# A streaming encoder step: unit 0's product block by block, and six low halves moved from GpSimd to VectorE

## The reference, cut to what matters

```
h = RMSNorm(x); z = h @ w_in                      # 9216 columns: GLU a, b, q, k, v, two gates
conv branch: GLU, causal depthwise conv 31, LayerNorm, swish, @ w_conv_out
attention:   8 heads, differential, QK-RMSNorm, rotary, block-causal mask, @ w_attn_out
x = x + (sigmoid(gate_conv) * conv + sigmoid(gate_attn) * attn) @ w_out
h2 = RMSNorm(x); q = h2 @ w_pq                    # 8 heads x 128
s1, s2 = q halves against 128 keys each           # top 16 of each, top 16 of the 256 sums
y = x + sum over the 16 chosen of softmax(score) * gelu(h2 . u_tab[idx]) * v_tab[idx]
```

## Time and profile before

| | |
|---|---|
| median of 3 runs | 4030.99 us (4030.02 to 4040.12) |
| the profiled execution, its own time | 4019.61 us |
| its span | 4017.8 us |
| mean granted TensorE clock | 0.981 of full |
| TensorE matmuls busy | 3831.1 us, 95% |
| VectorE busy | 3046.7 us, 76% |
| ScalarE busy | 1099.1 us, 27% |
| GpSimd busy | 1364.6 us, 34% |

### The profile page before, as it was taken

The page is one execution under the profiler, slowest core; times in us unless marked ns, Lnnn a source line. Parts: engine busy times, 40 slices in busy tenths (PEclk is TensorE's granted clock), DMA queues, the critical chain, the costliest instruction groups (busy, mean ns, idle before and its releaser), DMA issues.

```text
span 4017.8 us, 67592 instructions
## 1 busy us (share of the span) xinstructions
PE 3831.1 (95%) x24995; PEld 3772.7 (94%) x24995; DVE 3046.7 (76%) x3852; ACT 1099.1 (27%) x1126; POOL 1364.6 (34%) x947
## 2 busy tenths in 40 slices
PE   8989989989989998999999999999999999999999
PEld 7889889988989998998999999999999999999999
DVE  6887887788776424188668999998678888888876
ACT  3223222222323112132223333333222222222222
POOL 3333333333334442466652222222223333233320
PEclk9999999999989999999999999999999999999999
DMA  7998999989978997786759999999979888889895
GB/s 283 320 347 316 322 321 327 330 306 338 350 267 294 324 329 251 253 294 229 242 214 352 383 386 389 382 387 380 355 272 357 338 334 337 341 321 347 330 355 188
DMA packets 451684, 1285.17 MB, mean 320 GB/s; under 512 B 34368, under 2 KB 258368, under 8 KB 343360
## 3 DMA queue, kind: packets, MB, share of 16 engines
q1 hardware_dynamic: 372576, 876.99, 61.5%
q0 software_dynamic: 46080, 335.56, 21.2%
q10 hardware_dynamic: 32832, 70.07, 4.5%
HBM read 1070.18 MB, written 345.75 MB: 352 GB/s over the span
## 4 chain that ended last, share of the span: by engine, by line
PE 51%; issue 15%; DMA 13%; DVE 11%; POOL 5%; SPq 3%; ACT 1%; DVEq 1%; POOLq 0%; ACTq 0%
PE ST L1889 18%; PE ST L1800 17%; PE PA L1560 13%; DMA u_rows<-u_out 6%; POOL w_lo L622 5%; DMA w_raw<-w_all 4%; DVE xg L1069 4%; DMA rows<-v_rows,v_idx 2%; PE ST L1865 2%; DVE u_out L968 2%; SPq L393 1%; DVE w_lo L1364 1%; DVE PA L1459 1%; ACT w_hi L677 1%; DMA rows<-u_rows,v_idx 1%
## 5 line engine op out<-in xcount | busy, mean ns | idle before, releaser
L622 POOL TENSOR_TENSOR w_lo<-w_raw,w_hi 128x512 fp32r<-128x512 f32 x612 | 838.3, 1402 | 1223.4 <-ACT w_hi L677 1223.4
L677 ACT ACTIVATE w_hi<-w_raw 128x2048 fp32r<-128x2048 f32 x368 | 703.6, 1912 | 1307.3 <-PE ST L1889 507.2
L1889 PE MATMUL ST<-wt_hi,w_hi 128*128 128x384 f32 x2048 | 686.9, 335 | 15.2 <-DVE w_lo L1364 15.1
L1889 PE MATMUL ST<-wt_lo,w_hi 128*128 128x384 f32 x2048 | 684.7, 334 | 0.0
L1889 PE MATMUL ST<-wt_hi,w_lo 128*128 128x384 f32 x2048 | 684.7, 334 | 0.0
L1364 DVE TENSOR_TENSOR w_lo<-w_raw,w_hi 128x2048 fp32r<-128x2048 f32 x213 | 487.1, 2287 | 174.1 <-ACT w_hi L677 166.8
L650 POOL DMA_INDIRECT rows<-v_rows,v_idx x160 | 322.9, 2018 | 739.3 <-DVE PA L1459 670.2
L1560 PE MATMUL PA<-h_hi,w_hi 128*128 128x272 f32 x2496 | 547.8, 301 | 6.4 <-POOL w_lo L622 6.4
L1560 PE MATMUL PA<-h_hi,w_lo 128*128 128x272 f32 x2496 | 527.1, 293 | 0.0
L1560 PE MATMUL PA<-h_lo,w_hi 128*128 128x272 f32 x2496 | 527.1, 293 | 0.0
L1800 PE MATMUL ST<-h_hi,w_hi 128*128 128x384 f32 x1408 | 508.5, 361 | 2.2 <-ACT h_b L875 1.6
(11 more groups left out here) (271 smaller groups left out, 6190.6 us busy)
## 6 DMA issues: line engine op xcount, KB each, us to landing
w_raw<-w_all SPq DMA_DIRECT2D x368, 1024.0 KB
u_in<-w_all SPq DMA_DIRECT2D x128, 1024.0 KB, 8.7
u_rows<-u_out SPq DMA_DIRECT2D x512, 256.0 KB, 7.5
v_rows<-w_all SPq DMA_DIRECT2D x128, 1024.0 KB, 9.2
a_scr<-gb ACTq DMA_DIRECT2D x128, 192.0 KB
g_scr<-g_st ACTq DMA_DIRECT2D x24, 1024.0 KB, 11.9
gl_st<-g_scr SPq DMA_DIRECT2D x30, 768.0 KB
a_st<-a_scr SPq DMA_DIRECT2D x30, 768.0 KB
```

The lines of the kernel that those rows point to most:

```text
L622: ins = pool.tensor_tensor(w_lo[:, slot, cols], raw[:, slot, cols], w_hi[:, slot, cols].bitcast(F32), ALU.subtract)
L677: act.activation(w_hi[:, slot, :], raw[:, slot, :], ACT.Copy).then_inc(hi_ready, 1)
L1889: last = mm(PB[n % 2][:, k, :], a, r_[b][:, c, :], start=(c == 0 and y == 0), stop=(c == GRP - 1 and y == 2))
```

## The change

At the start: SyncE's queue loads the constants behind the first piece of x and unit 0; ScalarE's queue keeps parameters and lambdas, with a semaphore of their own, and makes one small copy ahead of the data. GpSimd no longer makes squares or low halves there: ScalarE makes the even squares, VectorE the odd ones and the low halves of units 0 and 1. TensorE starts unit 0 once its low half and the first `h_lo` are there, waits per block, and takes the sums of squares in four lots, behind blocks 4, 8, 11 and 13. The hooks `stats` and `rot` of the first head move one quarter of a unit later. Later: VectorE makes the low half of the third query unit behind its first two copies, and in each top-k tile that of the last unit (7), between the multiply and the reduction of list 0. GpSimd's loops are cut at these units.

```diff
@@ SyncE
             for i in range(4):
                 sp.dma_start(xs[:, 4 * i:4 * i + 4, :], x_t[:, 4 * i:4 * i + 4, :]).then_inc(x_loaded[i], 16)
-                if i == 1:
+                if i == 0:
                     load_w(0, 0)
+                    sp.dma_start(cst[:, :], consts).then_inc(const_loaded, 16)
             load_w(0, 1)
@@ GpSimd
-            for k in range(1, KD, 2):
-                pool.wait_ge(x_loaded[k // 4], 16)
-                pool.tensor_tensor(xsq[:, k, :], xs[:, k, :], xs[:, k, :], ALU.mult).then_inc(xsq_pool, 1)
-                if k == KD // 2 - 1:
-                    lo_whole(0, 0)
-            lo_whole(1, 1)
...
+            pool.wait_ge(lo_ready, 2)
+            made = 0
+            for w0, w1 in ((2, U_PQ + 2), (U_PQ + 3, U_PU + TOPK_UNITS - 1), *((U_PU + TOPK_UNITS * t, U_PU + TOPK_UNITS * (t + 1) - 1)
+                                                                   for t in range(1, TT)), (U_PU + TOPK_UNITS * TT, U_PU + U_G0 + 1)):
+                pool.wait_ge(lo_ready, w0)
...
@@ ScalarE
-            for dst, src in ((cst, consts), (par, params)):
-                act.dma_start(dst[:, :], src).then_inc(const_loaded, 16)
-            act.dma_start(lam_sb[:, :, :], lams).then_inc(const_loaded, 16)
+            act.dma_start(par[:, :], params).then_inc(par_loaded, 16)
+            act.dma_start(lam_sb[:, :, :], lams).then_inc(par_loaded, 16)
+            act.wait_ge(u_zeroed, 1)
+            act.activation(a_t[:, 0:1], u[:, 0:1], ACT.Copy)
...
-                if k % 4 == 0:
-                    act.activation(xsq[:, k, :], xs[:, k, :], ACT.Square).then_inc(xsq_act, 1)
-                if k == KD // 2 - 1:
+                if k == 3:
                     hi(0, 0)
+                if k >= 3:
+                    for j in range(0 if k == 3 else k, k + 1):
+                        if j % 2 == 0:
+                            act.activation(xsq[:, j, :], xs[:, j, :], ACT.Square).then_inc(xsq_act, 1)
@@ VectorE
             for k in range(KD):
...
                 dve.wait_ge(xhi_ready, k + 1)
                 V.scalar_tensor_tensor(h_lo[:, k, :], xs[:, k, :], par[:, P_G1 + k:P_G1 + k + 1],
                                        h_hi[:, k, :].bitcast(F32), ALU.mult, ALU.subtract).then_inc(xlo_ready, 1)
+                if k == 3:
+                    split(0, 0)
+                if k >= 3:
+                    for j in range(0 if k == 3 else k, k + 1):
+                        if j % 2:
+                            V.tensor_tensor(xsq[:, j, :], xs[:, j, :], xs[:, j, :], ALU.mult).then_inc(xsq_dve, 1)
+            split(1, 1)
...
+            query(0)
+            split(U_PQ + 2, 0)
+            with dve.Fori(1, NQ // 2) as v:
+                query(v)
...
                                            .broadcast_to([P, NH, TOPK, TOPK]), ALU.mult))
                     settle()
+                    if s == 0:
+                        split(U_PU + TOPK_UNITS * (tt + 1) - 1, 1)
                     ins = V.tensor_reduce(isel[:, s, :], wk[:, :].rearrange("p (x a) -> p x a", a=TOPK), AX.X, ALU.add)
@@ TensorE
+            def x_stats(k0):
+                for k in range(k0, k0 + 4):
+                    pe.wait_ge(xsq_dve if k % 2 else xsq_act, k // 2 + 1)
+                    last = spread(S, ones, xsq[:, k, :], start=(k == 0), stop=(k == KD - 1))
+                if k0 == KD - 4:
+                    last.then_inc(stat_ready, 1)
+
+            def first_unit(k):
+
+                if k == 4:
+                    pe.wait_ge(const_loaded, 16)
+                if k in (4, 8, 11, 13):
+                    x_stats({4: 0, 8: 4, 11: 8, 13: 12}[k])
+                if k < KD - 1:
+                    pe.wait_ge(xlo_ready, k + 2)
...
-                at = {(1, 1): lambda: stats(h, 0), (1, 2): lambda: rot(h, 0),
+                at = {(1, 2 if h == 0 else 1): lambda: stats(h, 0), (1, 3 if h == 0 else 2): lambda: rot(h, 0),
```

More of the change, by code:

```diff
@@ L297, in build @@
         x_loaded = [sem(f"x_loaded{i}") for i in range(4)]
-        xsq_act, xsq_pool, xsq_dve = sem("xsq_act"), sem("xsq_pool"), sem("xsq_dve")
+        xsq_act, xsq_dve, par_loaded = sem("xsq_act"), sem("xsq_dve"), sem("par_loaded")
         xhi_ready, xlo_ready, lam_ready, u_zeroed = sem("xhi_ready"), sem("xlo_ready"), sem("lam_ready"), sem("u_zeroed")
@@ L610, in _ @@
             pool.memset(u[:, 0:HIST], 0.0).then_inc(u_zeroed, 1)
[L612 to L615, removed]
             def lo(w, slot, nth):
@@ L627, in lo @@
                         ins.then_inc(lo_ready, 1)
-            for k in range(1, KD, 2):
-                pool.wait_ge(x_loaded[k // 4], 16)
-                pool.tensor_tensor(xsq[:, k, :], xs[:, k, :], xs[:, k, :], ALU.mult).then_inc(xsq_pool, 1)
-                if k == KD // 2 - 1:
-                    lo_whole(0, 0)
-            lo_whole(1, 1)
[L635 to L643, removed]
+            pool.wait_ge(lo_ready, 2)
[3 more added lines that the diff above has]
+                pool.wait_ge(lo_ready, w0)
+                w = w0
+                if w % 2:
+                    lo(w, 1, 3 * made + 3)
+                    w, made = w + 1, made + 1
+                pairs = (w1 - w) // 2
+                if pairs:
+                    with pool.Fori(0, pairs) as v:
+                        for n in range(2):
+                            lo(v * 2 + (n + w), n, v * 6 + 3 * (made + n + 1))
+                w, made = w + 2 * pairs, made + 2 * pairs
+                if w < w1:
+                    lo(w, 0, 3 * made + 3)
+                    made += 1
             def fetch(j):
@@ L677, in hi @@
                 act.activation(w_hi[:, slot, :], raw[:, slot, :], ACT.Copy).then_inc(hi_ready, 1)
-            act.wait_ge(const_loaded, 48)
+            act.wait_ge(par_loaded, 32)
             for k in range(KD):
@@ L943, in _, with split @@
             settle()
-            dve.wait_ge(const_loaded, 48)
+            dve.wait_ge(par_loaded, 32)
+            def split(un, slot):
+                dve.wait_ge(hi_ready, un + 1)
+                dve.wait_ge(lo_ready, un)
+                V.tensor_tensor(w_lo[:, slot, :], raw[:, slot, :], w_hi[:, slot, :].bitcast(F32), ALU.subtract)\
+                    .then_inc(lo_ready, 1)
             for k in range(KD):
-                if k % 4 == 2:
-                    dve.wait_ge(x_loaded[k // 4], 16)
-                    V.tensor_tensor(xsq[:, k, :], xs[:, k, :], xs[:, k, :], ALU.mult).then_inc(xsq_dve, 1)
                 dve.wait_ge(xhi_ready, k + 1)
@@ L1234, in _, with query @@
                         .then_inc(h2_ready, 1)
-            with dve.Fori(0, NQ // 2) as v:
+            def query(v):
                 for n in range(2):
@@ L1359, in one_hot @@
                 ins.then_inc(oh_ready, 1)
[L1361 to L1365, removed]
             def dot(v, i, h2_rows=h2_g):
@@ L1686, in _ @@
                         pe.wait_ge(zb_full, un + 1)
-                        product(PV[n % 2], n % 2, 0, range(KD), h_hi, h_lo, order(hooks, i)).then_inc(unit_done, 1)
+                        now = order(hooks, i)
+                        if un == 0:
+                            pe.wait_ge(xlo_ready, 1)
+                            now = {k: lambda k=k: first_unit(k) for k in range(KD)}
+                        product(PV[n % 2], n % 2, 0, range(KD), h_hi, h_lo, now).then_inc(unit_done, 1)
             pe.wait_ge(zb_full, NZ + 1)
```

## The result

| | before | after |
|---|---|---|
| median | 4025.69 us (4015.08 to 4040.12, 14 runs) | 4040.77 us (4034.12 to 4046.11, 14 runs) |
| ratio, 95% interval | | 1.0036 [1.0026, 1.0046] |
| profiled execution: own time, span | 4019.61, 4017.8 us | 4037.16, 4035.4 us |
| granted clock, mean | 0.981 | 0.979 |

The change made the kernel 15 us slower. The forecast was +2.8 us (4034, range 4019 to 4044): the time lies in the range, but 12 us of loss had not been counted, and the 0.36% is more than the 0.3% that a measurement tells from no change. The range was drawn about 4031.0, the median that the kernel before had then; here it has 4025.7. Counted from the kernel before, the range ends at +13, and the change cost 15: that the time falls inside is in part luck.

What follows compares the result with a forecast made beforehand. TensorE's matmuls fill 95% of the span, so edits were priced where it stands still: −8.0 −2.7 −5.6 +12.5 +6.6 = +2.8 on 4019.6, 4022.4, plus 11.4 to the runs' median: 4034 us, range 4019 to 4044.

Steps and rivals of the forecast that it cites:

- Part 1: The start: unit 0 begins at 14.2 us, last sums end at 33.1 instead of 39.5; −8.0 us, bounds −4.4 and −9.
- Sixteen sums of squares in four lots of 2.10 are 8.4: At the start: TensorE's time for all sums, putting the last lot's end at 14.2+10.5+8.4 = 33.1 us.
- The step from 6.4 to −8.0: Start: sums end 6.4 us earlier, ScalarE's square root 8.3 earlier, the DMA stream has some 1.8 us of air; taken as −8.0.
- Part 2: Third query unit: VectorE makes its low half, TensorE starts at 1610.6 instead of 1613.26; −2.7 us, bounds −1.5 and −4.5.
- Part 3, tiles 2 to 4: Last three top-k tiles: VectorE's wait makes the choice late, +12.5 us; half clock behind three stops, +6.6, bounds 0 and +8.
- Part 3, tiles 0 and 1: First two top-k tiles, no turning: unit 6's half ready sooner, −1.6 and −4.0, together −5.6 us, bounds −8 and −2.
- the −1.6: Top-k tile 0: the next tile's first unit starts at 1767.9 instead of 1769.45 us.
- A: Rival, top-k tiles: the choice isn't late, the wait costs TensorE nothing; −25, 4006 us; chance 0.12.
- B: Rival, start: unit 0 runs at half clock, start costs +10 instead of −8; total +21, 4052 us; chance 0.07.
- The sign that the prediction gave for B or C: Start: first sums ending after 38 us, the two told apart by granted clock and h_lo's mean.
- C: Rival: the start gives nothing, h_lo staying at 1.65 us on average, sums at 39; +11, 4042 us; chance 0.07.
- D: Rival, top-k tiles: GpSimd's new loop boundaries wait for VectorE's halves and hold up later ones; +8, 4042 us; chance 0.03.

Runs made afterwards that it cites:

- kernel 5: Kernel before with the new start alone, third query unit's and top-k halves left with GpSimd: 4030.23 us, ratio 0.9992 [0.9980, 1.0004].
- kernel 12: Kernel before with the new start alone, all sums of squares behind block 1 instead of in four lots: 4016.21 us, ratio 0.9975 [0.9959, 0.9991].
- kernel 8: Changed kernel with sums of squares over only 8 of the 16 blocks (norm of half the channels): 4036.86 us, ratio 1.0013 [1.0002, 1.0025].
- kernel 10: Changed kernel with VectorE making unit 6's half instead of unit 7's, and all sums of squares behind block 1: 4008.12 us, ratio 0.9951 [0.9935, 0.9966].
- 9: Changed kernel with VectorE making unit 6's low half instead of unit 7's in the top-k tiles: 4015.17 us, ratio 0.9971 [0.9961, 0.9982].
- Kernel 3: Changed kernel with all four lots of sums of squares behind block 1 of unit 0: 4040.77 us, ratio 1.0031 [1.0018, 1.0044].
- kernel 4: Changed kernel where VectorE only waits for unit 7's high half at the same place and GpSimd makes the low half: 4036.02 us, ratio 1.0015 [1.0002, 1.0028].
- kernel 2: Changed kernel with VectorE's low half of unit 7 moved behind the choice in each tile: 4031.13 us, ratio 0.9994 [0.9980, 1.0007].
- Kernel 7: Kernel before with VectorE making the third query unit's half and, in each top-k tile, unit 6's half: 4014.44 us, ratio 0.9968 [0.9952, 0.9983].
- kernel 6: Kernel before with the top-k part alone, VectorE making unit 7's half between multiply and reduction of list 0: 4049.38 us, ratio 1.0046 [1.0030, 1.0061].
- kernels 1: Changed kernel with the top-k part undone, GpSimd making unit 7's low half in all five tiles: 4022.77 us, ratio 0.9993 [0.9981, 1.0004].
- kernel 11: Kernel before with one edit, VectorE making the third query unit's half: 4025.62 us, ratio 0.9998 [0.9983, 1.0012].

## Why the prediction was right or wrong

**Part 1 failed in one term.** "Sixteen sums of squares in four lots of 2.10 are 8.4": the row that this rests on is of eight instructions, and eight are two blocks, not four (64 instructions of `ST<-xsq` stand for the sixteen blocks in after; a block has two halves of 272 columns and each takes two). A lot is 3.83 us. Four times 1.73 is 6.9 of the 8.7 us between 33.1 and 41.8. Another 0.3 is the later start, and most of the rest is that the first pairs of unit 0's matmuls take 0.66 us in place of 0.41. These are rows of after:

```profile
15.15 0.66 PE L1575 MATMUL PA<-h_lo,w_hi 128*128 128x272 f32 x2
...
18.70 0.41 PE L1575 MATMUL PA<-h_hi,w_hi 128*128 128x272 f32 x2
...
1614.50 0.66 PE L1575 MATMUL PA<-h_lo,w_hi 128*128 128x272 f32 x2
```

The column of the granted clock reads 1.00 at 15, but 0.66 is what the same pair takes at 1614.50, where it reads 0.50. So it was half clock here as well; it cost 1.9 us (14.54 to 18.70 for nine pairs that later start every 0.25 us).

So the sums end 2.3 us later than before, SyncE's loads go out later too, and the part is worth −3 us [−8, +2] (kernel 5) in place of −8.0. The step behind it, that an earlier end of the sums lasts to the end, is borne out by three kernels of four: with the sums ending at 32.6 the start gives −10 us (kernel 12), with half of them 9 less than after (kernel 8), and 7 on top of the best tiles (kernel 10 against 9). Only kernel 3, 2 us under after by two ratios whose intervals are ±5 and ±4, leans the other way. The single profiles misled here, since the stretch up to the merge differs by up to 16 us between kernels with the same code for it.

The count could have been made before: the number of instructions in a row has to be divided by what one block issues before a duration is carried over to a number of blocks. Two smaller slips stand in the working: 51.5 less 34.7 is 16.8, not 16.5, and the upper bounds of the parts add up to +12.6, not +11; neither moves the forecast. The step from 6.4 to −8.0 was taken without a sum; kernel 12's −10, good to ±6 us, neither shows nor refutes it.

**Part 2 was right**: −2.7 forecast, −2.6 in after's profile. The half clock after the wait stayed.

**Part 3, tiles 2 to 4, was right in mechanism and sum, not in the shares**: +12.5 and +6.6 are 19.1, and the three tiles cost 19.5. The mechanism, the wait for a high half that comes only after unit 5, is shown from two sides: the wait without the work costs 14.2 in these tiles (kernel 4), the work without the wait 5.2 in the profile of all five and nothing by the ratio (kernel 2). Kernel 7, where the operand is ready, agrees. The shares show in what TensorE did between the marks of the table above, in us, summed over the matmuls; "lost" is half of the time in which it worked at a granted clock of 0.50:

| tiles | idle, before and after | lost at half clock, before and after |
|---|---|---|
| 0 | 4.6, 4.5 | 1.7, 1.7 |
| 1 | 6.2, 6.0 | 1.7, 4.6 |
| 2 to 4 | 13.8, 29.8 | 3.4, 6.8 |

In tiles 2 to 4 idle time gives +16.0 where +12.5 was forecast, and the clock +3.4 where +6.6 was. After's 6.8 is the size that was forecast, but the kernel before lost 3.4 there too, behind its stops of 2.9 us for unit 6's half, and the prediction counted no half clock in it. That the two errors cancel to 0.4 us is luck.

**Part 3, tiles 0 and 1, was wrong by 7.8**: −5.6 forecast, +2.2 measured, and +2.3, +2.4 and −0.3 in kernels 6, 8 and 3, which have the same edit. In tile 0 the forecast of its own row came true, and yet nothing was gained. TensorE began tile 1 in after here:

```profile
1768.59 0.44 PE L1825 MATMUL PA<-h_hi,w_hi 128*128 128x384 f32 x1 [1.96 <-POOL w_lo L618]
```

Before it was 1769.45, and the shift there is +0.7: −1.6, as forecast. But TensorE had 2 us of idle time just ahead of it, where before it had none, since now unit 7 was ready early and ended early. What follows is these two windows of after, and then the same stretch of before:

```profile
1765.00:1770.00 5.00, 3.04 (x25) 2.75 (x22) 3.19 (x7) 0.76 (x1) 5.00 (x5) 0.96 0.20 48
1770.00:1775.00 5.00, 5.00 (x23) 5.00 (x22) 4.97 (x33) 0.00 (x0) 3.42 (x3) 0.70 0.80 289
```

```profile
1770.00:1775.00 5.00, 5.00 (x31) 5.00 (x30) 4.97 (x18) 0.00 (x0) 3.75 (x3) 1.00 0.85 266
```

A clock of 0.70 for 5 us is 1.5 us: the −1.6 is gone. The kernel before had paid the same earlier in the tile, behind its stop for unit 6's half:

```profile
1747.65 0.45 PE L1800 MATMUL PA<-h_hi,w_hi 128*128 128x384 f32 x1 [2.79 <-POOL w_lo L622]
```

```profile
1748.00:1752.00 4.00, 4.00 (x16) 4.00 (x15) 3.97 (x2) 0.48 (x1) 4.00 (x2) 0.57 0.84 270
```

So the −1.6 at 1768.59 was a half clock that before had behind it and after still ahead; over the tile both lose 1.7 us to the clock, and the idle time is the same within 0.1. The prediction read one place and took none of this into account: idle time and half clock were moved, not removed.

In tile 1 the idle time is about the same too (6.2 and 6.0), and the loss is in the clock. VectorE's compare and multiply met GpSimd at unit 5's half, which was then late, and TensorE stood for it:

```profile
1806.94 3.27 DVE L1343 TENSOR_TENSOR wk<-jf,late_sb 128x2048 f32<-128x2048 f32 x1
1810.25 3.27 DVE L1347 TENSOR_TENSOR wk<-wk,tif 128x2048 f32<-128x2048 f32 x1
1828.65 2.29 DVE L951 TENSOR_TENSOR w_lo<-w_raw,w_hi 128x2048 fp32r<-128x2048 f32 x1 [15.13 <-ACT w_hi L677]
```

```profile
1806.70 14.11 POOL L618 TENSOR_TENSOR w_lo<-w_raw,w_hi 128x512 fp32r<-128x512 f32 x8 [3.46 <-ACT w_hi L677]
```

```profile
1815.99 0.44 PE L1825 MATMUL PA<-h_hi,w_hi 128*128 128x384 f32 x1 [3.27 <-POOL w_lo L618]
```

Eight quarters took GpSimd 14.11 us (units 5 and 6), beside 9.91 for eight with no compare or multiply next to them in tile 0. The clock is at 0.65 in 1818 to 1822, behind this stop, and at 0.50 in 1850 to 1855, behind the next one of 2.71 us. The working took tile 1 as of tile 0's pattern; VectorE's place against the units is another in each tile, and that has to be read for each. That it is the idle time of VectorE which does the harm in these tiles is not shown: kernel 4 keeps the wait and loses nothing in the two of them. Nor is the kernel before's profile a steady base for tile 1: it and kernel 5 stand 5.0 us for unit 6's half there, kernels 1, 11 and 12 with the same tiles 2.9, and these are 3.6 to 3.7 us shorter.

**The sum.** With the start taken by its ratio, the parts are −3 −2.6 +2.2 +19.5 = +16.1 where the forecast had +2.8. By ratios alone, −3 (kernel 5), −1 (kernel 11) and +18.5 (kernel 6) add to +14.5, and 14.5 us is what 1.0036 says. After's own profile shows +22.5 at the end of the top-k stage and gives 4.9 back in that of v_tab; that is not steady (kernel 6 gives back 0.8, kernel 8 5.3), and its cause stays open.

**Rivals.** A, the choice isn't late, is refuted by the 22.2 us of stops. B, unit 0 at half clock, came true for 4 us of the 19 that it needed, and cost 1.9 us; from 18.7 on the pairs take 0.41. The sign that the prediction gave for B or C, sums ending after 38 us, was met by neither of them but by the wrong count. C said that the start gives nothing, and near nothing it gave, but by another cause: h_lo ran at 0.78. D: after's loops hold nothing up; kernels 7, 9 and 10 run with such loops and gain.

## What to carry to other kernels

A piece of work that is moved to a less busy engine needs its operand at the place where it stands in that engine's order, not only room there: ask for each place when the operand is ready and what is queued behind it. Here one unit earlier turned +22 us into −11 (against one profile of before; unchanged tiles lie between 0 and −5), in part because TensorE had stood for that unit's half. When idle time in front of TensorE is shortened, split or moved, count the half clock behind the stops in both kernels, those that go and those that come, over the whole stage and not at one place. A duration of joined instructions is carried over only with their count, and stretches in which profiles of the same code differ by many us are judged by timed ratios, each part by itself.

## What the runs showed of the hardware

- Short idle times of TensorE were followed by half clock in some places and not in others. In after the clock was 0.70 in the 5 us behind the 1.96 us of tile 0, and in kernel 7 it was 1.2 GHz behind the stop of 2.66 us in tile 2, but 1.00 from 1983 to 1988 behind the 2.64 us of tile 3. Kernel 7 in tile 2, then the kernel before in tile 3, where a stop of 2.89 us had no half clock behind it:

```profile
1907.00:1909.00 2.00, 2.00 (x8) 2.00 (x7) 0.00 (x0) 1.41 (x2) 0.14 (x1) 0.50 0.31 49
```

```profile
1981.43 0.44 PE L1800 MATMUL PA<-h_hi,w_hi 128*128 128x384 f32 x1 [2.89 <-POOL w_lo L622]
```

```profile
1980.00:1985.00 5.00, 3.57 (x20) 3.57 (x21) 4.93 (x3) 2.15 (x2) 5.00 (x3) 1.00 0.56 182
```

- At the start the first eight pairs of matmuls took 0.66 us each (the first 0.82) and those from 18.70 on 0.41, while the column of the granted clock read 1.00. 0.66 is the pair's time where the column reads 0.50, so the column doesn't show the half clock of TensorE's first 4 us; the duration of a row does.
- The first 1560 us, with the DMA engines at 0.83 to 0.97 of their time in stretches of 200 us, differ between profiles of the same code by up to 16 us, the unchanged top-k stage by up to 5. In that stage TensorE lost 6.8 us to half clock in the kernel before and 3.4 in kernel 12, and its idle time was 24.6 and 22.5 us: nearly all of the difference.
